# Gated linear attention stage: four PSUM banks instead of eight, score masks one tile ahead, block diagonal states, output norm on ACT and POOL

## What is computed

```python
def gla_chunk(S, q, k, v, lg):
    b = jnp.cumsum(lg, axis=1)
    o_inter = jnp.einsum('bthd,bhde->bthe', q * jnp.exp(b), S)
    diff = b[:, :, None] - b[:, None, :]
    decay = jnp.exp(jnp.where(causal, diff, -jnp.inf))
    A = jnp.einsum('bthd,btshd,bshd->bths', q, decay, k)
    o = o_inter + jnp.einsum('bths,bshe->bthe', A, v)
    b_last = b[:, -1]
    S_new = jnp.exp(b_last)[..., None] * S + jnp.einsum('bshd,bshe->bhde', k * jnp.exp(b_last[:, None] - b), v)
    return S_new, o
# merge_out:
    og = rms_norm(o_g, gla_norm_w).reshape(B, T, GLA_WIDTH) * jax.nn.silu(gg.astype(jnp.float32))
```

## Time and profile before

| what | value |
|---|---|
| timed runs | 1192.83 and 1195.55 us, median 1194.19 us |
| profiled execution, its own time | 1189.06 us |
| its span | 1187.4 us |
| mean granted TensorE clock, share of full | 0.954 |
| busy over the span: PE, DVE, ACT, POOL | 88%, 48%, 39%, 22% |

### The profile page before, as it was taken

How to read it: one execution, slowest core, us unless ns; L and a number is a source line. 1 busy time by engine, 2 the same in 40 slices (tenths; PEclk the granted TensorE clock), 3 DMA queues, 4 the chain that set the end, 5 groups by cost and what they waited for, 6 DMA issues and landing times. The chain is left out here.

```text
span 1187.4 us, 26574 instructions
## 1 busy us (share of the span) xinstructions
PE 1042.8 (88%) x9099; PEld 843.7 (71%) x9099; DVE 571.8 (48%) x1434; ACT 464.0 (39%) x1327; POOL 259.7 (22%) x416
## 2 busy tenths in 40 slices
PE   4999999999999999888899999556685899989988
PEld 3899999967677775666676776345564688778755
DVE  4755533434352331342434342379866766666422
ACT  5633312433442322332333443235424654554321
POOL 0000100012222221221222234399401111111200
PEclk9999999999999999999999999868885799999989
DMA  6423645479897865775898887561104122211101
GB/s 187 126 86 95 202 143 181 143 247 322 306 316 244 280 222 163 257 227 180 280 306 297 284 262 239 155 236 53 54 9 120 36 94 83 71 37 56 53 23 43
DMA packets 109433, 199.44 MB, mean 168 GB/s; under 512 B 15050, under 2 KB 49300, under 8 KB 109300
## 3 DMA queue, kind: packets, MB, share of 16 engines
q1 hardware_dynamic: 73892, 117.23, 31.8%
q0 software_dynamic: 20480, 67.13, 16.5%
q10 hardware_dynamic: 14928, 13.38, 3.4%
HBM read 178.87 MB, written 19.60 MB: 167 GB/s over the span
## 5 line engine op out<-in xcount | busy, mean ns | idle before, releaser
L259 POOL DMA_DIRECT2D vraw<-in_cache_v x256 | 138.0, 539 | 615.6 <-issue 611.3
L1061 PE MATMUL bank<-wh,xTh 128*128 128x256 f32 (+1 forms) x864 | 252.2, 292 | 11.9 <-DVE qwr L1269 9.8
L1061 PE MATMUL bank<-wh,xTl 128*128 128x256 f32 (+1 forms) x864 | 244.9, 283 | 0.0
L1061 PE MATMUL bank<-wl,xTh 128*128 128x256 f32 (+1 forms) x864 | 244.7, 283 | 0.0
L477 DVE COPY kt<-bank 128x512 f32<-128x512 f32 x128 | 88.6, 692 | 182.8 <-PE bank L280 118.8
L1061 PEld LDWEIGHTS bank<-wh,xTh 128*128 128x128 f32 (+1 forms) x864 | 161.7, 187 | 20.3 <-DVE qwr L1269 11.6
L1061 PEld LDWEIGHTS bank<-wh,xTl 128*128 128x128 f32 (+1 forms) x864 | 161.3, 187 | 0.0
L1061 PEld LDWEIGHTS bank<-wl,xTh 128*128 128x128 f32 (+1 forms) x864 | 161.1, 186 | 0.0
L280 PE MATMUL bank<-ident,kraw 128*128 128x128 f32 x1024 | 153.3, 279 | 0.4 <-DVE kt L477 0.3
L401 ACT ACTIVATE kt<-bank 128x512 f32<-128x512 f32 x128 | 76.2, 595 | 158.8 <-PE bank L280 158.2
L280 PEld LDWEIGHTS bank<-ident,kraw 128*128 128x128 f32 x1024 | 112.8, 141 | 22.5 <-issue 21.6
(11 more groups left out here) (241 smaller groups left out, 1827.8 us busy)
## 6 DMA issues: line engine op xcount, KB each, us to landing
vraw<-in_cache_v POOLq DMA_DIRECT2D x256, 256.0 KB, 4.6
kraw<-in_cache_k SPq DMA_DIRECT2D x256, 256.0 KB, 4.0
wraw<-in_w_in SPq DMA_DIRECT2D x28, 512.0 KB, 4.9
out<-nat ACTq DMA_DIRECT2D x32, 128.0 KB, 2.2
wo_raw<-in_w_out SPq DMA_DIRECT2D x8, 512.0 KB, 9.3
xr<-in_x_prompt SPq DMA_DIRECT2D x7, 512.0 KB, 3.6
out<-xr SPq DMA_DIRECT2D x7, 512.0 KB, 2.6
bT<-in_x_prompt SPq DMA_DIRECT2D x4, 512.0 KB, 4.6
```

Of the source, the lines that this page charges most:

```text
L259: pool.dma_start(vraw[:, p % VR, :], cache_v.rearrange("a n p h d -> (a n) p (h d)")[bass.ds(page, 1)] .rearrange("o p c -> (o p) c")).the ...
L1061: ins = pe.matmul(z_at(u)[0:r, 0:CB], a[:, k, P * i:P * i + r], b[:, wslot(c), k, :], start=(n == 0), stop=(n == 3 * KT - 1))
```

## The change

In the GLA block:

- Scores use two banks (both groups write the same two), outputs one, and one bank, `pX`, serves turned keys, state increments and turned mixes in turn. `products` and `masks` are called per group, and masks of tile i+1 stand in iteration i of DVE's loop, after state(i-1).
- The states `sp_` and `ss_` become twice as wide, as a block diagonal of two heads with zeros elsewhere (POOL writes the zeros first). One matmul of 256 columns then takes the queries of two heads times their states, so `qz` goes.
- The norm's root is applied by ACT: `out(i)` squares straight from PSUM, makes the roots, and copies with four scaled copies; `norm(i)` is one multiply on POOL.
- `turn_k`, `turned_k`, `mixed` and `state` change their places, since they share `pX`. The loads of values and gates go from SP to ACT's queue; the states go in and out by one transfer for each head (twice as many issues). The stores of states are waited for before the next block's load of `vd`.
- The code that could place steps of the cached attention between GLA's steps is there, but `G_FIRST` and `G_EACH` are 0, so `PAUSE` is `NSUB` as before and none is placed there.

```diff
-        PAUSE = NSUB
+        G_FIRST, G_EACH = 0, 0
+        PAUSE = NSUB - G_FIRST - G_EACH * 6 * (TILES - 1)
...
-            pA = bank[:, 0:4, :]
-            pOg, pK, pdS, pM = bank[:, 4, :], bank[:, 5, :], bank[:, 6, :], bank[:, 7, :]
+            pA, pOg, pX = bank[:, 0:2, :], bank[:, 2, :], bank[:, 3, :]
...
+                def turn_k(i):
+                    r = rows_of(i)
+                    if i >= 2:
+                        pe.wait_ge(mgo, i - 1)
...
                 def state(i):
                     r = rows_of(i)
-                    pe.wait_ge(kdo, i + 1)
-                    if i >= 1:
-                        pe.wait_ge(sdn, i)
+                    pe.wait_ge(kdo, min(i + 2, TILES))
+                    if i == TILES - 1:
+                        pe.wait_ge(mgo, i)
...
                 def out(i):
 
                     r = rows_of(i)
                     act.wait_ge(ogd, i + 1)
+                    for h in range(H):
+                        c = slice(h * DV, (h + 1) * DV)
+                        ins = act.activation(squares_g[0:r, c], pOg[0:r, c], ACT.Square, accum_out=r4g[0:r, 0, h:h + 1])
+                    linked(ins)
+                    linked(act.activation(r4g[0:r, 1, :], r4g[0:r, 0, :], ACT.Ln, scale=1.0 / DV, bias=eps_g[0:r, :]))
+                    linked(act.activation(r4g[0:r, 2, :], r4g[0:r, 1, :], ACT.Exp, scale=-0.5))
                     if i >= 1:
                         act.wait_ge(mgd, i)
-                    act.activation(og[0:r, :], pOg[0:r, :], ACT.Copy).then_inc(ogc, 1)
...
+                        ins = act.activation(og[0:r, c], pOg[0:r, c], ACT.Copy, scale=r4g[0:r, 2, h:h + 1])
+                    ins.then_inc(ogc, 1)
...
+                def norm(i):
+                    r = rows_of(i)
+                    pool.wait_ge(ggd, i + 1)
+                    pool.wait_ge(ogc, i + 1)
+                    if i >= 1:
+                        pool.wait_ge(mgt, i)
+                    pool.tensor_tensor(mixg[0:r, :], og[0:r, :], gg[0:r, i % 2, :], ALU.mult).then_inc(mgd, 1)
...
+                for hh in range(2):
+                    off = (slice(DK * hh, DK * hh + DK), slice((1 - hh) * DV, (2 - hh) * DV))
+                    pool.memset(sp_[off[0], :, off[1]], 0.0).then_inc(off_zero, 1)
+                    pool.memset(ss_[off[0], :, :, off[1]], 0.0).then_inc(off_zero, 1)
```

More of the change, by code:

```diff
@@ L186, in hymba_kernel @@
         v_in = [sem(f"v_in{n}") for n in range(VR)]
+        v_late = [sem(f"v_late{n}") for n in range(2)]
         c_in = sem("c_in")
@@ L1341, in hymba_kernel @@
             at = g2.take("at", [P, 2, 2, 2, P])
-            kd = g2.take("kd", [P, 2, P])
-            q8 = g2.take("q8", [P, 2, 2, NB + 1, LASTW])
+            kd = g2.take("kd", [P, 2, 2, P])
+            q8 = g2.take("q8", [P, 2, NB + 1, LASTW])
             og = g2.take("og", [P, W])
@@ L1347, in hymba_kernel @@
             r4g = g2.take("r4g", [P, 3, 4])
-            qz = g2.take("qz", [P, 3, 2, 2, P])
             squares_g = nat[:].rearrange("p n c -> p (n c)")[:, 0:W]
@@ L1436, in _, with products @@
+                for h in range(H):
+                    half, c = slice(DK * (h % 2), DK * (h % 2) + DK), slice(h % 2 * DV, (h % 2 + 1) * DV)
+                    sp.dma_start(s_sample[0, :, h].rearrange("b d e -> d b e"), ss_[half, :, h // 2, c]).then_inc(g_out, 16)
+                    sp.dma_start(s_prompt[0, 0, h], sp_[half, h // 2, c]).then_inc(g_out, 16)
             @block.tensor
             def _(pe):
-                def products(i):
+                def products(i, g):
                     r = rows_of(i)
-                    pe.wait_ge(fdone, i + 1)
-                    for g, group in enumerate(level_groups(i)):
+                    if g == 0:
+                        pe.wait_ge(fdone, i + 1)
@@ L1453, in products @@
-                        ins.then_inc(adone, 1)
-                    if i >= 1:
-                        pe.wait_ge(kdo, i)
+                            pe.wait_ge(amask, groups_done(i - 1, 1))
+                    else:
+                        pe.wait_ge(amask, groups_done(i, 0))
+                    for n in level_groups(i)[g]:
+                        s1, t0 = (HALVES[0], HALVES[0]) if n == 0 else (r, 0)
+                        for h in range(H):
+                            half = slice(DK * (h % 2), DK * (h % 2) + DK)
+                            c0 = (n % 2) * 256 + (h // 2) * P
+                            ins = pe.matmul(pA[0:s1, h % 2, c0 + t0:c0 + r],
+                                            ff[half, i % 3, n, 1, h // 2, 0:s1],
+                                            ff[half, i % 3, n, 0, h // 2, t0:r], start=True, stop=True)
@@ L1656, in _, with factors @@
                 exponents(pool, linked, 1)
-                pool.wait_ge(g_in, 16 * 7)
+                exponents(pool, linked, 2)
+                pool.wait_ge(g_in, 16 * 9)
                 for i in range(TILES):
-                    if i + 2 < TILES:
-                        exponents(pool, linked, i + 2)
+                    if i + 3 < TILES:
+                        exponents(pool, linked, i + 3)
                     gate(i)
+                    norm(i)
             @block.vector
             def _(dve):
-                def factors(i):
+                def factors(i, place):
@@ L1687, in masks @@
-                def masks(i):
+                            ins.then_inc(q8d, 1)
+                    else:
+                        ins.then_inc(fdone, 1)
+                def masks(i, g):
                     r = rows_of(i)
@@ new lines, in masks @@
+                    dve.wait_ge(adone, groups_done(i, g))
+                    for n in level_groups(i)[g]:
+                        if n == LV - 1:
+                            mk = (mask if r == P else mask8)[:, :].unsqueeze(1).unsqueeze(1)\
+                                .to_broadcast([r, 2, 2, r])
+                            every = slice(0, r)
+                            ins = dve.tensor_tensor(at[0:r, i % 2, :, :, 0:r], sums(n, every, every), mk, ALU.mult)
+                            if i < TILES - 1:
+                                ins.then_inc(diag_done, 1)
+                                dve.wait_ge(diag_done, i + 1)
+                            continue
+                        half = HALVES[n]
+                        for s0 in range(0, P, 2 * half):
+                            s, t = slice(s0, s0 + half), slice(s0 + half, s0 + 2 * half)
+                            ins = dve.tensor_copy(at[s, i % 2, :, :, t], sums(n, s, t))
```

291 lines of the change are left out of this document (154 added, 137 removed).

## The result

The changed kernel took 1248.19 us in the median of 2 runs (1246.60 to 1249.79), the kernel before 1194.19 us (1192.83 to 1195.55): ratio 1.0452, 95% interval 1.0375 to 1.0529, slower. The forecast was 1228, the range 1210 to 1246. The profiled execution has a span of 1248.1 us, 60.7 more than before.

| stretch | before, us | after, us | more | forecast |
|---|---|---|---|---|
| span's start to the GLA block | 765.79 | 770.57 | +4.8 | 0 |
| block's start to the first state | 30.22 | 40.32 | +10.1 | +9.5 |
| first state to state(7), seven tiles | 68.70 | 103.68 | +35.0 | +24.0 |
| state(7) to the first add of state(8) | 12.71 | 18.36 | +5.7 | +2.9 |
| the nine adds | 13.15 | 15.56 | +2.4 | 0 |

A forecast was written before the change was run, and what follows sets the result against it. It took a ring of waits through all engines, closed by the shared bank, to bound the GLA loop: tiles +24.0, start +9.5, last tile +2.9, end +2.9, so +39.3 on 1189.06 gives 1228 us, range 1210 to 1246.

The forecast's parts named there:

- What bounds the kernel: GLA tile loop: DVE set the pace before, 9.8 us a tile; after the change a ring of waits would.
- The ring: GLA tile loop: sharing one bank chains masks, products, output, ACT's norm and copies, transposes and state; 13.7 us a tile.
- The ring's price at either clock: GLA tile loop: one turn of waits through all engines costs 12.0 us at full TensorE clock, 16.2 at half.
- I take 40% at half: GLA tile loop: PE at half clock 40% of the time, so 13.7 us a tile, +24.0 us over seven.
- The last tile: State(7) to first add of state(8): output(8) 9.0 us, then PE waits for mixed(7) behind out(8); 15.6 us, +2.9.
- the adds: Nine adds of state(8) after the last tile: run 1.43 + 11.69 us as before, no change.
- The start: GLA block's start to first state: POOL's zeros delay exponents and masks(0), then steps at half clock; +9.5 us.
- the end: Last add to next block: eight store issues by SP where there were four; +2.9 us (0.4 to 6).
- The steps listed behind masks(0): Block start, at half clock: first masks, products, output(0), ACT, turned keys and state, reaching the first state at 805.5 us.
- rival 3: GLA tile loop: POOL sets the pace, blocked by DVE's multiplies, 12.3 us a tile; 1215 us, chance 6%.
- rival 2: GLA block: half clock nearly throughout, as PE waits in four places of each ring; +57, 1246 us, chance 15%.
- The forecast's range for its own case: Whole kernel: the main forecast of 1228 us, given 58%, runs from 1218 to 1238.

## Why the prediction was wrong, point by point

- **What bounds the kernel**: right. The ring was named arrow by arrow, and each wait of a measured turn is for the engine that it named. Own banks or another order open it and give back 4.4 to 5.2 us a tile, to 9.6 and 10.4 us, below even the 11.5 to 11.75 of the closed ring at full clock.
- **The ring's price at either clock**: right. 12.0 forecast at full, 11.51 to 11.75 measured at a clock of 1.00 (11.7 to 12.5 at 0.91); 16.2 at half, 15.8 to 16.1 in the slow turns, whose mean clock was 0.61 and not 0.50. Scaled copies from PSUM were 1.02 to 1.14 as priced, squares from PSUM cost nothing extra.
- **"I take 40% at half"**: the step that failed. It argued that no wait is as long as the 5.00 before and that the work is only a bit less dense. The waits are indeed short (at most 3.0 us in a tile, for the turned mixes), and still the granted clock was 0.67 in the profiled run and 0.63 in its repeat, 66% and 74% of the time at half. By the prediction's own terms 66% gives 12.0 + 0.66 x 4.2 = 14.8 a turn and 9.3 + 0.66 x 3.7 = 11.7 for the last, 100.5 us or +31.8 for the seven tiles, of the +35.0 measured, against +24.0. The 3.2 left is the second fault of that step: it weighted the ring by the mean clock, and the half clock lies where PE works. In the turn shown above 78% of the time was at half (clock 0.61), which gives 15.3 by that formula, and 15.84 came; the turns at 0.73 give 14.3, and 14.88 came. Over six turns these differences are 3.5 us; the last, shorter turn takes 0.2 back.
- **The last tile**, +2.9 against +5.7, and **the adds**, 0 against +2.4: both mis-sized by the same cause. I had taken output(8) and the increments at full clock; the first half of output(8) ran mostly at half (mean clock 0.68), the second at full, and the increments at half throughout. The sized idle matmuls brought them to 16.37 and 13.12, where the forecast had 15.6 and the old 13.15; 0.8 us of the 16.37 are the idle matmuls' own.
- **The start**, +9.5 against +10.1, and **the end**, +2.9 against +3.6: right in size. The start was right in its parts too: the zeros took 4.2 us for 4.1 (each half of the partitions gets 2304 of them, one after the other, so 4608 is their sum and not the number in each partition), and masks(0) began 22.65 us after the block's start for 22.6. The steps listed behind masks(0) add up to 17.5 and so to 805.9, +9.9, where +9.5 was written. I missed that a second cause, the late load of the states, stands ready when the zeros go.
- **POOL** (rival 3): not the bound at this pace, and its 11.4 us a tile was 11.1 where the ring was open, and it did set the pace there. **Half clock nearly throughout** (rival 2, 1246) came nearest: its +57 has +41.5 for the tiles where +35.0 was measured, and +3.5 for the last tile and adds where +8.1 was, so that it came near is in part two errors that cancel.

So the error of the sum is made up of 11.0 us in the tiles, 2.8 in the last tile, 2.4 in the adds, 0.6 at the start and 0.7 at the end, less 0.9 of the rest: 16.6, which is +55.9 measured from the block's start on less +39.3 forecast. The first three, 16.2 of it, hang on the clock, as the runs with idle matmuls show. The forecast's range for its own case ended at 1238, since a share above one half had been put into a rival of 15%.

## What to carry to other kernels

When a change gives one bank to three users, write down the ring of waits that it closes and price it at both clocks. The profile gives these prices well. What it doesn't give is the clock of the new loop, so carry both ends. In this case, with PE waiting in several places of each turn, the lower clock was the better guess; and the clock to charge is that in which PE works, not the mean of the turn. Before banks are bought back, look at the order: moving ACT's norm, and PE's outputs, behind the steps that the ring needs gave 38 of some 56 us (1248.53 to 1209.96) with the same four banks.

## What the runs showed that I had not expected

- The clock stayed down at short waits. In the changed kernel over the tiles no wait of PE is longer than 3.0 us, and the granted clock was 0.67; with 13 idle matmuls a tile in two of the gaps it was 0.91. And it stood at half while PE worked, at full while PE mostly waited.
- Some of POOL's small operations take five times as long beside DVE's long multiplies. With the zeros on DVE and the loads on SP, four subtractions of 128x64 on POOL, 0.29 us each when alone, took 1.5 each, the length of a multiply, while DVE multiplied 128x1280 from 780.97 to 787.1:

```profile
780.68 0.61 POOL L1672 TENSOR_TENSOR dd<-bT 128x256 f32<-128x256 f32 x1
781.25 1.54 POOL L1682 TENSOR_TENSOR dd<-bT 128x64 f32<-128x64 f32 x1
782.75 1.53 POOL L1683 TENSOR_TENSOR dd<-bT 128x64 f32<-128x64 f32 x1
```

- An idle matmul of 128 columns cost 0.24 us at full clock (22 in 5.18 us) and 0.31 in a row that began at half (30 in 9.25), so filling a wait needs its number worked out like any other work.
